# Asking for the next step's cache pages between the two halves of a step's rearranging transfers

## What is computed

```python
def step(carry, phys):
    c_blk = cache_ckv[layer, phys]
    kp_blk = cache_kpe[layer, phys]
    kn_blk, v_blk = _decompress(c_blk, w_ukv, g_kn)
    return _merge(carry, _attn_partial(qn, qp, kn_blk, kp_blk, v_blk, None)), None

carry, _ = lax.scan(step, init, page_table.T)
```

## Time and profile before

| what | us |
|---|---|
| median of 3 runs | 1269.84 |
| lowest and highest run | 1267.92 and 1271.21 |
| the profiled execution, its own time | 1272.07 |
| its span in the trace | 1270.3 |
| TensorE busy in the span | 1200.1 |
| VectorE busy | 732.2 |
| ScalarE busy | 426.9 |
| GpSimd busy | 258.1 |

### The profile page before, as it was taken

The page is one execution under the profiler, slowest core; times in us unless marked ns, Lnnn a source line. Parts: engine busy times, 40 slices in busy tenths (PEclk is TensorE's granted clock), DMA queues, the critical chain, the costliest instruction groups (busy, mean ns, idle before and its releaser), DMA issues.

```text
span 1270.3 us, 23638 instructions
## 1 busy us (share of the span) xinstructions
PE 1200.1 (94%) x8783; PEld 660.5 (52%) x8783; DVE 732.2 (58%) x1801; ACT 426.9 (34%) x1041; POOL 258.1 (20%) x294
## 2 busy tenths in 40 slices
PE   6999999989999999999989989999999999989898
PEld 3545677845555565654534445555444444454343
DVE  4000437865667666774768788887766676430321
ACT  3000354333343333342545334333434344210310
POOL 0000134721011121234413340012232332000000
PEclk9999999999999999998999999999999999989999
DMA  6413112123232322351452226523566554101000
GB/s 220 168 55 87 35 34 67 51 63 80 65 83 68 77 72 78 88 111 46 131 146 77 76 80 175 175 73 83 152 182 168 138 127 115 47 1 38 17 21 33
DMA packets 205236, 114.45 MB, mean 90 GB/s; under 512 B 152977, under 2 KB 196433, under 8 KB 204994
## 3 DMA queue, kind: packets, MB, share of 16 engines
q1 hardware_dynamic: 198482, 96.56, 27.7%
q0 software_dynamic: 4352, 10.49, 3.0%
q10 hardware_dynamic: 2288, 5.89, 1.3%
HBM read 75.79 MB, written 4.07 MB: 63 GB/s over the span
## 4 chain that ended last, share of the span: by engine, by line
PE 71%; DVE 10%; SPq 8%; issue 5%; DMA 4%; ACT 2%; another core or an unknown queue 1%; POOL 1%; DVEq 0%; ACTq 0%
PE PS L615 20%; PE PS L1604 8%; PE PS L1442 7%; SPq L503 7%; PE PS L2816 4%; PE PS L2846 4%; PE PS L1758 3%; DMA c_ring<-in_cache_ckv 3%; PE PS L582 2%; PE PS L599 1%; DVE ssq L738 1%; PE PS L2859 1%; PE PS L578 1%; PE PS L2399 1%; PE PS L2768 1%
## 5 line engine op out<-in xcount | busy, mean ns | idle before, releaser
L615 PE MATMUL PS<-wk,c_T 128*128 128x512 f32 x1024 | 494.4, 612 | 13.2 <-DVE c_T L725 12.1
L615 PEld LDWEIGHTS PS<-wk,c_T 128*128 128x128 f32 x1024 | 180.4, 194 | 207.6 <-issue 163.5
L738 DVE TENSOR_REDUCE ssq<-PS 128x8 f32<-128x512 f32 x256 | 176.3, 688 | 166.3 <-ACT PS L661 149.3
L661 ACT ACTIVATE PS<-PS 128x512 f32<-128x512 f32 x256 | 150.4, 588 | 270.4 <-PE PS L615 240.0
L1604 PE MATMUL PS<-xnT,w_ring 128*128 128x276 f32 x416 | 102.7, 404 | 0.0
L1442 PE MATMUL PS<-w_ring,xnT 128*128 128x424 f32 x256 | 95.8, 531 | 0.9 <-DVE xnT L1089 0.9
L725 DVE STREAM_TRANSPOSE c_T<-blocks 128x512 f32<-128x512 f32 x126 | 88.3, 701 | 5.2 <-DMA blocks<-c_ring 4.9
L1604 PEld LDWEIGHTS PS<-xnT,w_ring 128*128 128x128 f32 x416 | 78.9, 192 | 21.2 <-issue 4.1
L541 POOL DMA_INDIRECT c_ring<-in_cache_ckv,token_rows x48 | 45.5, 947 | 182.7 <-PE PS L599 175.3
L532 POOL DMA_INDIRECT r_ring<-in_cache_kpe,group_rows x64 | 62.2, 972 | 89.2 <-DVE r_T L733 73.0
L1442 PEld LDWEIGHTS PS<-w_ring,xnT 128*128 128x128 f32 x256 | 48.7, 194 | 45.4 <-issue 45.4
(11 more groups left out here) (535 smaller groups left out, 1722.5 us busy)
## 6 DMA issues: line engine op xcount, KB each, us to landing
blocks<-c_ring SPq DMA_DIRECT2D x504, 64.0 KB
c_ring<-in_cache_ckv SPq DMA_DIRECT2D x208, 128.0 KB, 2.2
w_ring<-in_w_in SPq DMA_DIRECT2D x4, 1696.0 KB, 12.3
w_ring<-in_w_in SPq DMA_DIRECT2D x9, 512.0 KB, 5.0
w_o<-in_w_out SPq DMA_DIRECT2D x8, 512.0 KB, 4.9
w_g<-in_w_ple_gate SPq DMA_DIRECT2D x8, 512.0 KB
xn<-in_x_prompt SPq DMA_DIRECT2D x4, 512.0 KB, 10.8
w_ring<-in_w_in SPq DMA_DIRECT2D x2, 1024.0 KB, 6.3
```

Of the source, the lines that this page charges most:

```text
L615: mm = pe.matmul(PS[:, NORM[v % 2], :], c_T[:, u % 2, k, t * P:(t + 1) * P], wk[:, k], start=(k == 0), stop=(k == 1))
L661: nc.scalar.activation(PS[:, NORM[v % 2], :], PS[:, NORM[v % 2], :], ACT.Square).then_inc(no_sb, 1)
L738: dve.tensor_reduce(ssq[:, u % 2, t * H:(t + 1) * H], PS[:, NORM[v % 2], :].rearrange("p (h c) -> p h c", h=H), AX.X, ALU.add).then_inc(re ...
```

## The change

pages(u+1) now stands between blocks(u, 0) and blocks(u, 1) on SP. Before, pages(u) stood ahead of both halves of its own step. The pieces are cut anew: the first piece of a step is now blocks(u, 0) alone; the second is page numbers(u+1), the wait for `vv_ps`, pages(u+1), and blocks(u, 1). So blocks(u, 0) comes a piece earlier against SP's other work, and pages(u+1) comes ahead of blocks(u, 1), with its wait for the values of step u-3. The number of transfers and what they move is the same, and so are the programs of the four other engines. Lines behind the edit move down by 5.

```diff
         def pages_sp():
             sp = nc.sync
-            for u in range(NSTEP):
+
+            def pages_of(u):
                 page = page_numbers(u)
                 if u >= RING:
                     sp.wait_ge(vv_ps, u - RING + 1)
                     sp.sem_inc(slot_taken, 1)
-                if u >= ahead_pages:
-                    latent_pages(u, page)
-                yield
+                latent_pages(u, page)
+
+            for u in range(NSTEP):
                 if u >= 1:
                     if u >= 2:
                         sp.wait_ge(lo_sb, u - 1)
                     blocks_of(u, 0)
+                yield
+                if ahead_pages <= u + 1 < NSTEP:
+                    pages_of(u + 1)
+                if u >= 1:
                     if u >= 2:
                         sp.wait_ge(hi_sb, u - 1)
                     blocks_of(u, 1)
```

## The result

The changed kernel took **1279.66 us** (median of 7 runs, 1278.11 to 1284.17), the kernel before, run beside it, 1271.13 (7 runs, 1267.92 to 1274.45): a ratio of 1.0079, 95% interval 1.0064 to 1.0094, so 0.8% slower. (The ratios here come from all runs and not from the two medians, whose quotient is 1.0067.) The prediction was 1268.6, range 1265.0 to 1273.0. It was wrong.

A forecast was written before the change was run, and what follows sets the result against it. The prediction took SP's chain of issues and page landings to bound the tail, TensorE's work nearly everywhere else. Tail -2.4 plus step 25 +1.2 gave -1.2 us, from 1269.84 to 1268.6 us, range 1265.0 to 1273.0.

The forecast's parts named there:

- the floor: Tail: steps cannot go below 9.035 us, the pace TensorE, ScalarE and VectorE set one another through two PSUM banks.
- The plain steps: Tail steps without a weight load: from 9.21 us towards 9.035, with the room taking up issues that run long.
- The loaded steps: Ten tail steps with a 512 KB load: 0.1 to 0.6 us to spare, three or four late, about 0.9 in all.
- the slower rival: Second halves land late, up to 9.77 us per loaded step; tail about +4, step 25 +5, total 1275; chance 0.17.
- the sign that the prediction had named for late halves: VectorE idle before each transpose of a second half in the loaded steps, and those steps over 9.3 us.
- Its threshold of 3.1 us: Tail: late second halves would decide the outcome from a landing time of about 3.1 us.
- The tail together: All 19 tail steps: -3.3 gain plus 0.9 for late loaded steps, -2.4 us; bounds -3.3 and +4.
- The forecast's upper bound: Whole kernel: +1.6 us, from -1.0 for the tail and +2.6 for step 25.
- Step 25: Before the tail: transpose and `wuq` load both 1.1 to 1.6 us later, costing once, +1.2 us; bounds +0.4 and +2.6.
- The wait for the values of step u-3: SP's wait ahead of the pages (L599): values end at 894.11, number reads about 894.5, so it costs nothing.
- The other early steps: Outside the tail, except step 25: second halves issued some us later, nothing lost; least room 1.3 us, at step 24.
- The median: Whole kernel: forecast counted from a median of 1269.84 us for the kernel before.

The follow-up runs named there:

- tail_loads_after: Changed kernel with the new order only in the tail (old order up to step 41) and the tail's ten weight loads behind the second halves: 1267.96 us, ratio 0.9979 to before.
- tail_only: Changed kernel with the new order only in the tail, steps 42 to 63, and the old order before it: 1271.03 us, ratio 1.0011 to the kernel before.
- not_25: Changed kernel with the old order kept in steps 24 and 25, new order everywhere else: 1272.75 us, ratio 1.0013 to the kernel before.
- numbers_early: Changed kernel with the page numbers of u+1 read ahead of blocks(u, 0) instead of ahead of the pages: 1277.58 us, ratio 1.0049 to the kernel before.
- small_ahead: Changed kernel with only 16 of 1024 columns of each tail weight load ahead of the pages, the rest behind the second half: 1277.14 us, ratio 1.0048 to before.
- loads_after: Changed kernel with the tail's ten weight loads moved three slots later, behind the second half: 1275.84 us, ratio 1.0044 to the kernel before.
- six_stores_out: Changed kernel without the six sample-state stores between the halves of step 25 (outputs not written): 1271.94 us, ratio 1.0004 to the kernel before.
- both_mended: Changed kernel with the old order in steps 24 and 25 and the tail's loads behind the second halves: 1268.84 us, ratio 0.9977 to the kernel before.

## Why the prediction was wrong, point by point

- **What bounds the kernel, and the floor: right.** The tail was SP's chain, the floor is 9.035. Nine plain steps at 9.04, and with the loads moved the other ten at 9.06 to 9.10. SP's 30 us of waiting were worth some 3 us, no more; tail_loads_after brought the steps to that floor.
- **The plain steps: right**, -1.0, against -1.6 for the nine by the prediction's mean of 9.21 for all steps (the plain ones had been at 9.14).
- **The loaded steps: the mechanism of the slower rival, smaller than its price.** Two sizes failed. The forecast took a landing of 1.65 to 2.18 us for a half behind the load; it was 2.4 to 3.5. And it took the pages' landing as hidden in every step; in the loaded ones SP waited 14.7 us for pages, as much as before, so that a half's last issue ended 9.1 us in the mean after the first transpose of the step before, where the forecast's sums give 8.4. Every one of the ten halves was waited for, the sign that the prediction had named for late halves, and the steps lost 2.7 us in this profile instead of gaining 1.7 less 0.9 = 0.8. The rival had 3.7 for the landing and 9.77 for the step, where 9.54 were measured. Its threshold of 3.1 us doesn't follow from its own sums, by which the half is late from 2.2 on (10.68 - 8.46) and the step is longer than before from 2.6; so less was needed for it than the prediction said, and the landing times that the forecast used came from halves with no load ahead. The Trainium skill ("DMA: Bandwidth & Descriptors", "Queues, rings and completion order") has the descriptors of a queue taken in ring order on each DMA engine. The step times are in line with that, 9.54 us with 512 KB ahead of pages and half and 9.15 with 8 KB, but no run separates the order in the queue from a plain sharing of the DMA engines by transfers in flight together.
- **The tail together:** -2.4 forecast, +1.7 measured between steps 44 and 63, and +0.9 and -0.5 in tail_only and not_25, which have the same order there. The forecast's upper bound took -1.0 for the tail, a figure that its working doesn't give.
- **Step 25: the term that failed, +1.2 forecast, +6.4 measured.** The place, the instructions ahead of the half and the event that ends the wait were as told. Their sizes were not: what stands ahead of the second half on SP was put too short. Its last issue was put at 639.3 to 639.8 and ended at 643.81. All items missed on the same side, 4.2 us in sum, by the rows of SP above: the second half of step 24 and the first of step 25 took 3.39 and 3.40 us where 2.7 had been put; the stores 4.32, not 3.9; from the last store to the first page, with its four number reads, 2.8, not 0.94; and the pages ahead of all this went out at 620.70, not 620.22. I had taken the durations of a quiet queue, for the reads those of the tail, where there are two in a step. `wuq`, behind the same items, came late by as much, so that the two did cost once, as forecast, but 6 us and not 1.2. The upper bound, +2.6, was made by putting back one of them only (the stores).
- **The wait for the values of step u-3: right.** It ended at 631.55, ahead of the stores' end. SP waits there in other steps (83.6 us in 32 of them by the page of waits) without making anything late.
- **The clock: missing from the sum.** 1.6 of the 6.4 us on the chain come from it (at full clock TensorE would have waited for `wuq` during some 0.7 of them): beside an idle time of 5 us stands a stretch at the lower level, in after, in numbers_early (5.16 us idle), in small_ahead (5.15) and in loads_after (4.80, with 0.52 and 0.50 granted over the 7 us from 641.0; there the lower level began 2.4 us into the idle time, in the other three about at its end). In the five kernels whose half came in time there, tail_only, tail_loads_after, not_25, six_stores_out and both_mended, the granted clock stays at 1.00 from 636 to 652. So the four kernels with the idle time have the lower level and the five without it have not.
- **The other early steps: right in the result, close in the margin.** The second halves go out mostly 3 to 8 us later, and none is waited for. But the room at step 24 was 0.4 us (landed 628.50, transposed from 628.88), not 1.3.
- **The median:** the forecast was made from 1269.84, the kernel before ran at 1271.13 beside the changed one; of the 11 us between forecast and result this is 1.3.

What stays open: why the issues and reads at step 25 took longer than on a quiet queue, and why the lower-clock stretches at 571, 603 and 755 us come and go between kernels. They move single profiles by 1 to 3 us and so some of the last microsecond in every comparison here.

## What to carry to other kernels

When transfers change places on one engine's queue, add up what stands ahead of each transfer at the fullest place, with the durations measured there and not the shortest ones seen elsewhere; where all terms can only err upwards, the sum needs an upper bound that takes all of them together. A large load just ahead of small, urgent transfers on the same queue cost by its bytes here, not by its issue; putting it behind was worth 0.27 to 0.43 us in each of ten steps. And an order that helps in one stage need not stand in all: applied in the tail alone, with the loads behind, this change gained 0.2%, where the new order everywhere, with the loads where they were, lost 0.8%.

## What the hardware showed that I had not expected

- The same instruction on SP varied by a factor of three: the read of a page number took 0.26 to 0.94 us at step 25, and one of the four transfers of a half at 623 took 1.34 us where 0.62 is usual. I didn't find what sets it.
- A 512 KB load took 0.61 us to issue ahead of the pages (937.88) and 0.42 behind two of them.
- The granted clock of TensorE fell to 0.54 in the 3.6 us after an idle time of 5.1 us that ended a stretch of full clock.
